# Moving the z projection into the pauses of the state-space steps, with earlier activation tables and filler products at the norms

## What is computed

```
def even_mixer(...):
    z, xbc, dt_f, dt_b, q, k, v, r, gl_f, gl_b = split_cols(h @ w_in, EV_SPLITS)
    xbc = silu(centred_conv(xbc, conv_w, conv_b))
    ssd_c, ssd_l = bidirectional(ssd_scan, ...)
    y = (y_ssd + d_skip[:, None] * xs) * silu(z)
    y = rms_norm(y.reshape(b, t, SSD_GROUPS, ...), ssd_nw)
    o = rms_norm(y_gla, gla_nw) * silu(r)
    return concatenate([y, o], axis=-1) @ w_out

h = rms_norm(x, norm) * (1 + sc) + sh          # before each mixer and each feed-forward
x = x + g1 * mixer(h);  x = x + g2 * swiglu(h')
```

## Time and profile of the kernel before

| what | value |
|---|---|
| median of the runs | 2292.64 us (3 runs, 2291.91 to 2293.5) |
| the profiled execution's own time | 2295.65 us |
| its span, first to last instruction | 2293.8 us |
| mean granted TensorE clock | 0.947 of full speed |
| busy: PE, DVE, ACT, POOL | 91%, 32%, 25%, 3% of the span |
| chain that ended last | PE 81%, DVE 11%, ACT 5% |

### The profile page before, as it was taken

One profiled execution on the slowest core, in us unless ns is written; L12 is line 12 of the kernel. 1 busy time (PEld: TensorE's weight loads), 2 busy tenths in 40 slices (PEclk: granted clock), 3 DMA queues, 4 the chain that ended last, 5 costly groups with the idle time before them and its releaser, 6 DMA issues.

```text
span 2293.8 us, 29492 instructions
## 1 busy us (share of the span) xinstructions
PE 2089.5 (91%) x12486; PEld 1289.4 (56%) x12486; DVE 729.5 (32%) x1474; ACT 566.1 (25%) x1217; POOL 79.6 (3%) x86
## 2 busy tenths in 40 slices
PE   6999766999999799999999998999898889799997
PEld 2468443488555544444444446544576556578886
DVE  2540665000444500100000004555686944210001
ACT  4121112141334400200000004222536766420001
POOL 0000220000000000000000000000102110000000
PEclk9999887999989899999999997999998999799999
DMA  6333000312343122122221122221120001134442
GB/s 250 147 115 147 1 0 2 148 55 108 122 158 148 38 74 83 55 73 73 78 87 69 64 70 77 92 74 55 56 75 3 2 2 56 55 119 157 147 146 93
DMA packets 28000, 193.53 MB, mean 84 GB/s; under 512 B 3004, under 2 KB 4285, under 8 KB 5854
## 3 DMA queue, kind: packets, MB, share of 16 engines
q1 hardware_dynamic: 27826, 191.51, 22.7%
q10 hardware_dynamic: 44, 0.14, 0.0%
HBM read 190.59 MB, written 1.05 MB: 84 GB/s over the span
## 4 chain that ended last, share of the span: by engine, by line
PE 81%; DVE 11%; ACT 5%; issue 2%; DMA 1%; POOL 0%; SPq 0%; ACTq 0%; DVEq 0%; POOLq 0%
PE psum L673 80%; DVE ws_sb L1746 4%; ACT ws_sb L1312 2%; DVE gl_tmp_sb L1746 1%; DVE arena_sb L1746 1%; DVE hT_sb L1749 1%; ACT L1312 1%; ACT arena_sb L1312 1%; ACT wide_sb L1312 1%; DVE ws_sb L1749 1%; DMA xT_sb<-x 1%; DVE ring_sb L1746 1%; ACT const_sb L1312 1%; ACT hT_sb L1312 0%; DVE arena_sb L1755 0%
## 5 line engine op out<-in xcount | busy, mean ns | idle before, releaser
L673 PE MATMUL psum<-hT_sb,ring_sb 128*128 128x512 f32 (+1 forms) x2256 | 810.6, 522 | 19.4 <-ACT hT_sb L1312 15.0
L673 PEld LDWEIGHTS psum<-hT_sb,ring_sb 128*128 128x128 f32 x2256 | 433.7, 193 | 389.3 <-issue 357.0
L673 PE MATMUL psum<-arena_sb,ring_sb 128*128 128x512 f32 (+1 forms) x1216 | 396.3, 488 | 3.6 <-DVE small_sb L1752 1.9
L1312 ACT ACTIVATE ws_sb<-psum 128x512 f32<-128x512 f32 (+3 forms) x268 | 148.6, 554 | 860.8 <-PE psum L673 853.1
L673 PEld LDWEIGHTS psum<-arena_sb,ring_sb 128*128 128x128 f32 x1216 | 232.7, 192 | 165.3 <-issue 144.1
L673 PE MATMUL psum<-ring_sb,hT_sb 128*128 128x256 f32 (+4 forms) x1312 | 251.8, 378 | 11.3 <-ACT hT_sb L1312 11.3
L673 PEld LDWEIGHTS psum<-ring_sb,hT_sb 128*128 128x128 f32 (+1 forms) x1312 | 207.8, 187 | 56.9 <-issue 20.0
L673 PE MATMUL psum<-ws_sb 128*32 128x32 f32 (+5 forms) x2352 | 143.4, 234 | 46.8 <-DVE ws_sb L1746 46.4
L673 PEld LDWEIGHTS psum<-ws_sb 128*32 128x32 f32 (+4 forms) x2352 | 117.3, 134 | 86.3 <-DVE ws_sb L1746 60.3
L1746 DVE TENSOR_TENSOR arena_sb<-ws_sb,psum 128x512 f32<-128x512 f32 (+1 forms) x44 | 24.4, 555 | 419.9 <-PE psum L673 419.9
L1749 DVE SCALAR_TENSOR_TENSOR xT_sb<-psum,mod_sb,xT_sb 128x256 f32<-128x256 f32 x48 | 23.2, 484 | 388.3 <-PE psum L673 387.7
(11 more groups left out here) (154 smaller groups left out, 1404.7 us busy)
## 6 DMA issues: line engine op xcount, KB each, us to landing
ring_sb<-w SPq DMA_DIRECT2D x170, 1024.0 KB, 4.8
ring_sb<-w SPq DMA_DIRECT2D x8, 768.0 KB, 4.0
xT_sb<-x SPq DMA_DIRECT2D x1, 2048.0 KB, 14.0
const_sb<-consts SPq DMA_DIRECT2D x1, 2048.0 KB, 10.1
y<-xT_sb SPq DMA_DIRECT2D x1, 1024.0 KB, 4.8
ring_sb<-w SPq DMA_DIRECT2D x2, 256.0 KB, 4.1
const_sb<-consts SPq DMA_DIRECT2D x1, 512.0 KB, 5.7
const_sb<-consts SPq DMA_DIRECT2D x1, 384.0 KB
```

What stands on the lines that cost most here:

```text
L673: return nc.tensor.matmul(o, l, r, start=start, stop=stop)
L1312: return nc.scalar.activation(o, i, func, **kw)
```

## The change

The z block moves out of its own stage. Its 128 products become 32 parts of 4, one in each step of the SSD loop, into banks 2 and 3 (`z0_part`, `z_copy`). The off-diagonal and state products keep one bank each (1 and 0) in place of two. The q and k projection moves ahead of the loop, v0 begins straight after it, and the transposes of the SSD output come after v0. xdt and xw get a second buffer, and DVE's inputs for the next tile are made a step after the tile's first mask. The late halves are spread anew. At each norm a table load is issued early on ACT, ACT waits for the residual's bank semaphore directly, and PE runs five products of constants after the sums. The first group after a norm runs both output tiles chunk by chunk (`gemm_after`), small1 is merged with the first group of qkv, and beta's Sigmoid comes after Ln.

```diff
-LATE_AT = {"xbc": (0, 6), "z0": (6, 4), "qk0": (10, 4), "r0": (14, 2)}
+LATE_AT = {("xbc", 0): (0,), ("xbc", 1): (1,), ("xbc", 2): (2,), ("xbc", 3): (3,), ("xbc", 4): (4, 5), ("xbc", 5): (6, 7),
+           ("qk0", 0): (8,), ("qk0", 1): (9,), ("qk0", 2): (10,), ("qk0", 3): (11,),
+           ("r0", 0): (12,), ("r0", 1): (13,), ("r0", 2): (14,), ("r0", 3): (15,)}
...
     p.stage("small0", [([(64, KC)], 2)])
-    with_late("z0", 4)
     with_late("qk0", 4)
+    p.stage("z0", [([(CB, KC)], "z")] * 4)
     p.stage("v0", [([(CB, KC)], 2)] * 4)
...
-                if n == plan.stages["z0"][0][0][0]:
+                if n == plan.stages["qk0"][0][0][0]:
                     sp.dma_start(const[:, 6:NCONST - 1, :], consts[:, 6:NCONST - 1, :]).then_inc(s_levels, 16)
...
+            def gemm_after(stage, src, lo, tag):
...
+                for c in range(KC):
+                    chunk_ready(tag, c)
+                    for f in range(2):
+                        last = mm(psum[:, (first + f) % 4, lo:T], w[:, c, f * P:(f + 1) * P], src(c),
+                                  start=(c == 0), stop=(c == KC - 1))
+                        if c == KC - 1:
+                            last.then_inc(s_done, 1)
+                between(stage, 0)
...
+            def keep_clock(n):
+
+                for _ in range(n):
+                    mm(psum[:, 7, :], ones, cms("ident", 4).rearrange("p a b -> p (a b)"))
...
                 norm_sum(tag, KC - 1)
+                if tag != "fin":
+                    keep_clock(5)
...
+            def small1_and_first_queries():
...
+                for c in range(KC):
+                    chunk_ready("mix1", c)
+                    for j in range(TT):
+                        last = paired_mm(psum[:, 4 + j, 0:64], c, j, w[:, c, :])
...
+                    for f in range(2):
+                        last = mm(psum[:, (first + f) % 4, s], wq[:, c, f * P:(f + 1) * P], hT[:, c, s],
+                                  start=(c == 0), stop=(c == KC - 1))
...
+            def z0_part(n):
+
+                fill, sub = n // 4, n % 4
+                g, f, bank = fill // 2, fill % 2, 2 + fill % 2
...
+                if sub == 0:
+                    if f == 0:
+                        block_ready(block)
+                    if fill >= 2:
+                        pe.wait_ge(S["z_taken"], fill - 1)
+                j = 2 * f + sub // 2
+                for c in range(sub % 2 * 4, sub % 2 * 4 + 4):
+                    last = mm(psum[:, bank, sub // 2 * CB:(sub // 2 + 1) * CB], hT[:, c, j * P:(j + 1) * P], w[:, c, :],
+                              start=(c == 0), stop=(c == KC - 1))
...
             def ssd():
-                pe.wait_ge(S["late_copied"], 5)
-                pe.wait_ge(S["late_taken"], 4)
+                late_columns(5)
                 edges(0)
+                pe.wait_ge(S["late_taken"], 6)
...
+                z0_part(0)
+                z0_part(1)
                 pe.wait_ge(S["ssd_masked"], 4)
...
                     if u + 1 < 32:
                         decay(u + 1)
+                    if u + 2 < 32:
+                        z0_part(u + 2)
...
                     if hq == 1:
+                        if v > 0:
+                            pe.wait_ge(S["ssd_y"], v)
                         if k > 0:
-                            mm(psum[:, 2 + v % 2, :], cT[:, g, j * P:(j + 1) * P], st0[:, g])
-                        last = mm(psum[:, v % 2, :], b_tok[:, j, g * P:(g + 1) * P],
+                            mm(psum[:, 1, :], cT[:, g, j * P:(j + 1) * P], st0[:, g])
+                        last = mm(psum[:, 0, :], b_tok[:, j, g * P:(g + 1) * P],
...
             small0()
             for g in range(4):
-                gemm_tok("z0", g, (0, 1, 2, 3))
+                gemm("qk0", g, lambda c: hT[:, c, :], KC)
             ssd()
...
-            pe.wait_ge(S["ssd_y"], 16)
...
+            pe.wait_ge(S["ssd_exp"], 32)
+            pe.wait_ge(S["z_taken"], 8)
             for g in range(4):
                 gates(g)
+                if g == 1:
+                    pe.wait_ge(S["ssd_y"], 16)
                 gemm_tok("v0", g, (0, 1, 2, 3))
+            transpose_mix("ssd", y0, 8, TT)
...
# ACT
+            def load_tables(n):
+
+                nc.scalar.add_instruction(mybir.InstLoadActFuncSet(name=nc.get_next_instruction_name(), ins=[], outs=[], act_func_set_id=n))
...
                 n, h_before = NORM_AT[tag]
+                load_tables(LN_TABLES)
...
+                    if u % 4 == 3:
+                        z_copy(u // 4)
+                for i in range(2):
+                    z = z0[:, 2 * i:2 * i + 2]
+                    ins = f(z, z, ACT.Silu)
+                own(ins.then_inc(S["z_ready"], 1), S["z_ready"])
+                load_tables(LN_TABLES)
                 act.wait_ge(S["summed"], 1)
...
                 act.wait_ge(S["ab_raw"], 1)
-                link(f(beta, beta, ACT.Sigmoid))
                 log1p_exp_neg_abs(te, das, S["ab_ln"])
+                own(f(beta, beta, ACT.Sigmoid).then_inc(S["beta"], 1), S["beta"])
...
# DVE
+                inputs(0)
                 for u in range(32):
...
                     own(tt(p_seg[:, u % 2], e_seg[:, u % 2], bc(g_mask[:, d, g, TILE_AT[d][k]], 1, 4), ALU.mult).then_inc(S["ssd_p"], 1), S["ssd_p"])
-                    if u % 4 == 3:
+                    if u % 2 == 0 and u > 0:
                         accumulate(u // 2 - 1)
+                    if u % 4 == 1 and u < 28:
+                        inputs(u // 4 + 1)
```

More of the change, by code:

```diff
@@ L69 @@
 NCONST = 39
+LN_TABLES = 5
 NEAR = 6
@@ L193, in with_late @@
             groups += p.stages[name]
-            if g < n_late:
-                p.late.append(p.block("late", 2 * CB, KC // 2, None if (at + g) % 2 else 0))
+            for half in LATE_AT[name, g]:
+                p.late.append(p.block("late", 2 * CB, KC // 2, None if half % 2 else 0))
         p.stages[name] = groups
@@ L633, in backbone @@
         NORM_AT = {"mix0": (0, 0), "ffn0": (1, 16), "mix1": (2, 32), "ffn1": (3, 48), "fin": (4, 56)}
+        NORM_OF = {"ffn0": "out0", "mix1": "dn0", "ffn1": "out1", "fin": "dn1"}
         MIX_AT = {"ssd": (0, 0, 1), "gla": (8, 8, 2), "gdn": (16, 12, 1)}
@@ L711, in between, with gemm @@
             def between(stage, g):
[L713 to L719, removed]
+                for half in LATE_AT.get((stage, g), ()):
+                    late_half(half)
+            def gemm_after(stage, src, lo, tag):
+                ids, first = plan.stages[stage][0]
+                w = slot(ids[0], CB, KC)
+                block_ready(ids[0])
+                for f in range(2):
+                    bank_free(first + f)
+                for c in range(KC):
[6 more added lines that the diff above has]
+                between(stage, 0)
+            def gemm(stage, g, src, total, lo=0):
                 ids, first = plan.stages[stage][g]
@@ L834, in conv_stage @@
                 for g in range(info["tiles"] // 2):
-                    gemm(stage, g, lambda c, s=span(stage, 2 * g): hT[:, c, s], KC, lo=span(stage, 2 * g).start,
-                         after="mix0" if stage == "xbc" and g == 0 else None)
+                    src = lambda c, s=span(stage, 2 * g): hT[:, c, s]
+                    if g > 0:
+                        gemm(stage, g, src, KC, lo=span(stage, 2 * g).start)
+                    elif stage == "xbc":
+                        gemm_after(stage, src, 0, "mix0")
                     for t in (2 * g - 2, 2 * g - 1):
@@ L1390, in conv_stage @@
                         l2_scales(0)
[L1391 to L1392 removed]
+                    if stage == "xbc" and t in (3, 7, 9, 11):
+                        late_copy((3, 7, 9, 11).index(t))
                 activate(n_tiles - 1)
@@ L1854, in conv_stage @@
                         l2_scaled(0)
-                    if stage == "xbc" and t in (6, 10):
-                        late_taken(t // 4 - 1)
+                    if stage == "xbc" and t in (6, 9):
+                        late_taken(t // 9)
                 evac(info["tiles"] - 2)
```

151 lines of the change are left out of this document (78 added, 73 removed).

## The result

The changed kernel takes **2223.84 us** (median of 4 runs, 2220.2 to 2224.93), the kernel before beside it 2292.27 (2290.18 to 2293.5): ratio 0.970, 95% interval 0.9683 to 0.9716. The change saves 68.4 us; 74.7 were forecast, and 2223.84 lies in the range of 2202 to 2238.

What follows compares the result with a forecast made beforehand. TensorE, busy for 91% of the span, was taken to bound the kernel through its work, clock and waits. Terms -55.6 - 15.6 - 2.7 + 9.6 + 9.9 + 0.5 - 20.8 = -74.7 gave 2218 us, range 2202 to 2238.

Steps and rivals of the forecast that it cites:

- Part 1: z stage: it goes, -61.6 us, but four late halves and two column steps come back at 1.0 each: -55.6.
- slow restart in xbc: xbc: after the first wait for a weight block, products restart at a low clock, costing 2.7 us.
- Part 2: SSD stage with z inside: TensorE sets the loop's pace (133.6 us), stage 151 instead of 166.7: -15.6 us.
- the slow start put at 2.7: Start of the SSD stage: the clock is probably low after the edges' 16-column products, adding 2.7 us.
- (a): SSD loop: DVE and POOL slow each other, tiles stay at 20.2 us, 19 us more: 2237; chance 0.13.
- (e): SSD loop: each pair of steps becomes one serial chain, 16.7 us instead of 8.8: 2338; chance 0.03.
- Part 3: q and k projection: starts earlier, behind small0, without the slow restart: -2.7 us.
- Part 4: xbc and small0: doubled late halves delay weight blocks, waits of 3.8 and 3.1 plus a 2.7 restart: +9.6 us.
- Part 5: v0 straight after the loop: second gates wait 7.2 us for DVE, then a 2.7 slow restart: +9.9 us.
- chain of 23.2 us: Second gates: work queued from the SSD's end through gk takes 23.2 us against 16.0 of cover.
- Part 6: Norms: early table loads, fillers that hold the clock, and small1 merged with q: -20.8 us in all.
- Rival (b): Norms: fillers do not hold the clock; ffn0, ffn1 and mix1 lose 2.8 + 2.8 + 5: 2229; chance 0.08.

Runs made afterwards that it cites:

- the second profile: The changed kernel with nothing altered, profiled again in a later series: median 2225.7 us, ratio 0.9701 to the kernel before; this profiled execution took 2226.73 us.

## Why the prediction was right, and what its error is made of

**Part 1** (z goes, six short steps stay) was exact in kind. The 3.3 us missing in the row of small0 are not z: small0's 64 records of 32 columns took 11.78 us at clock 0.60, against 8.97 before, and the 16 records behind them 9.16 against 8.59. The prediction had put a slow restart in xbc (2.7; measured 1.7, 8.76 for 16 records at 0.69) and none on small0 behind the second wait. With no waits small0 took 8.03. A second profile of the kernel before had 11.08 with no wait in front, so the wait is not its only cause.

**Part 2** (the loop at TensorE's pace) held: 136.8 us with 134.0 busy, forecast 133.6 and 3.2 of wait at the end (2.78 measured). The stage's 151 were 148.3 and 150.7: the slow start put at 2.7 came in the second profile and hardly in the first. Rivals (a) and (e) needed masks that wait in each pair; inside the tile shown there is not a single wait. The experiments with the old order and with z first show what carried it: DVE's order, and with it z.

**Part 3** (q and k without slow restart, -2.7): in the trace after their groups take 14.00 us for 32 records, none slow; it is inside the row of small0.

**Part 4** (+3.8, +3.1, and a restart): 3.97 and 2.15, and the mechanism, three slots, was shown by moving it to r0 (5.01) and by hiding it (nothing). Blocks of small0's size landed in 2.7 us (median of two) and not in 4.1, which more than covers the 1 us too much.

**Part 5** (+7.2 and 2.7): 7.30 and 3.6 in the first profile. In the second PE came later, since its first gates and group ran slow (3.78 and 16.22 us), and waited 3.35; from gates to gates it is 23.3 us both times, because DVE's chain sets it. Taking the wait away gave 10.9 where the first gates ran at the full clock, and 5.5 where they ran slow, a case that the prediction did not have. The chain of 23.2 us on which its 7.2 rested was right. Where the stage is 2.4 and 4.3 shorter than forecast, 1.7 is a slow v0 group of the kernel before (64 records in 15.77 us, 14.08 at the full clock) that the prediction had overlooked; the rest was not looked for.

**Part 6**: ffn0 and mix1's norm -4.1 as forecast, ffn1 -2.9 against -3.0, 1.3 at the last norm, 2.18 us a merged chunk against 2.20 (small record 0.097, I took 0.11). Rival (b)'s price of 2229 less 2218, 11 us, was right by the median (11.3), which is in part luck: in the profile it gave 5 to mix1 where 15.1 were at stake, and 2.8 to each feed-forward stage where it is 1.7 and 1.8.

**The step that failed** is none of the six but the silent one beside them: stages that the change leaves alone were priced at nothing. GLA took 5.9 us more and the delta rule 2.8 in the second profile, 8.7 us together; small0's 3.3 comes on top, and the gates stage (4.3 less than forecast), the start (1.0) and small items give some back: 5.6 for the span, 6.3 for the median. That the total came so near is partly luck, since stages that ran over by 12.6 us met others that fell short by 7. In GLA it is granted clock on the same products. That the longer GLA comes with the change is likely (213.2 twice before, 214.5 to 219.0 in twelve profiles after), but what decides it stays open: no run isolated it, and the changed kernel itself shows two lengths. For the delta rule (551.7 and 552.7 before, 547.9 to 554.9 in the variants) not even the sign is certain.

## What to carry to other kernels

Moving work into an engine's pauses pays in full only if the engine that causes the pauses gets a new order as well: without the one or the other, 38 to 41 of the 68 us were gone. With a small ring of slots, count which transfer can start only at the end of the group that uses its slot, and put the extra blocks where something else hides it. Judge small edits by stage lengths in the trace, in profiles of the same kind, because stages that no edit touched moved the total by up to 10 us.

## What the runs showed that was not expected

- A pause's price depends on what follows it. After a pause of 4.6 to 4.8 us the half clock lasted about as long as a few wide products at ffn0 (1.7 us lost), but for 29 us with products of 64 columns among those of 256, PE busy throughout. Five filler products ahead of it, 4.46 us of otherwise idle time, were worth 15.1 us in these profiles; the medians give 11.3 for the fillers at all three norms.
- The fillers were worth so much only because of the merged loop; without both, mix1 lost 7.9 us and not 15.1.
- The same products in GLA took up to 5.9 us more through the granted clock alone (0.90 against 0.88). The kernel before repeated its length within 0.02 us (213.16 and 213.18), the changed one did not (215.65 and 219.01).
